# Sample sums by column ranges, conv transposes behind the last product, state transposes ahead of the last products

## The reference

```python
def merge_branches(x, o_cmp, o_sel, o_win, ng, o_fox, ga, gb, p):
    ...
    return x + jnp.einsum('bte,ed->btd', ga * ya + gb * yb, p['w_out'])

def conv_ffn(h, prev_rows, p):
    hn = rms_norm(h, p['norm_ffn_g'])
    u = jnp.einsum('btd,df->btf', hn, p['w_up'])
    g = jnp.einsum('btd,df->btf', hn, p['w_gate'])
    ...
    ue = jnp.concatenate([prev_rows.astype(u.dtype), u], axis=1)
    uc = p['conv_b'] + sum(p['conv_w'][k] * ue[:, k:k + T] for k in range(CONV_W))
    y = jnp.einsum('btf,fd->btd', jax.nn.gelu(uc) * g, p['w_down'])
    return h + y, ue[:, -(CONV_W - 1):]
```

## Time and profile before

| | |
|---|---|
| time, median of 3 runs | 892.27 us (892.04 to 892.54) |
| time of the profiled execution | 892.68 us |
| its span, first to last instruction | 890.8 us |
| mean granted TensorE clock | 0.978 of full |
| TensorE busy | 832.3 us |
| VectorE, ScalarE, GpSimd busy | 513.0, 366.5, 181.6 us |

### The profile page before, as it was taken

How to read it: one execution, slowest core, us unless ns; L and a number is a source line. 1 busy time by engine, 2 the same in 40 slices (tenths; PEclk the granted TensorE clock), 3 DMA queues, 4 the chain that set the end, 5 groups by cost and what they waited for, 6 DMA issues and landing times. The chain is left out here.

```text
span 890.8 us, 18476 instructions
## 1 busy us (share of the span) xinstructions
PE 832.3 (93%) x7479; PEld 682.0 (77%) x7479; DVE 513.0 (58%) x972; ACT 366.5 (41%) x660; POOL 181.6 (20%) x256
## 2 busy tenths in 40 slices
PE   6999887999999999989998788999799999999997
PEld 5999655899889876556554458995598899899885
DVE  6477688434437667635565424647666556656554
ACT  5246655423343244533243404425154344344332
POOL 3000385202210223333343500000011111101010
PEclk9999898999999999999999998999889999999999
DMA  6553495923443599999999988872074455554412
GB/s 204 178 165 120 78 306 206 245 96 104 174 155 139 176 408 356 326 406 390 422 416 395 398 316 229 225 273 94 0 236 143 142 158 194 185 170 141 141 47 64
DMA packets 90644, 192.07 MB, mean 216 GB/s; under 512 B 7467, under 2 KB 68811, under 8 KB 78060
## 3 DMA queue, kind: packets, MB, share of 16 engines
q0 software_dynamic: 15408, 106.04, 30.8%
q1 hardware_dynamic: 74878, 84.05, 30.4%
q10 hardware_dynamic: 288, 0.97, 0.4%
HBM read 187.57 MB, written 7.64 MB: 219 GB/s over the span
## 5 line engine op out<-in xcount | busy, mean ns | idle before, releaser
L1763 PEld LDWEIGHTS banks<-consts_base,stream_rows 128*128 128x128 f32 x672 | 73.2, 141 | 33.9 <-issue 26.9
L2002 ACT ACTIVATE keys_turned<-banks 128x512 f32<-128x512 f32 x94 | 55.1, 597 | 101.0 <-PE banks L1763 100.8
L1763 PE MATMUL banks<-consts_base,stream_rows 128*128 128x128 f32 x672 | 82.7, 276 | 7.4 <-DVE fox_probs_turned L1993 2.6
L261 PE MATMUL banks<-tokens_turned_high,w_gates_high 128*128 128x288 f32 x288 | 86.4, 300 | 2.3 <-PEq L194 2.3
L262 PE MATMUL banks<-tokens_turned_low,w_gates_high 128*128 128x288 f32 x288 | 85.3, 296 | 0.0
L263 PE MATMUL banks<-tokens_turned_high,w_gates_low 128*128 128x288 f32 x272 | 81.6, 300 | 0.0
L1296 PE MATMUL banks<-chunks_turned_high,cmp_w_high 64*128 64x256 f32 (+1 forms) x512 | 76.6, 293 | 3.0 <-ACT cmp_hidden L1390 2.6
L1296 PE MATMUL banks<-chunks_turned_low,cmp_w_high 64*128 64x256 f32 (+1 forms) x512 | 73.5, 280 | 0.0
L1983 DVE COPY keys_turned<-banks 128x512 f32<-128x512 f32 x74 | 50.4, 690 | 33.9 <-PE banks L1763 31.4
L254 DVE TENSOR_TENSOR chunks_turned_low<-banks,chunks_turned_high 128x512 fp32r<-128x512 f32 x64 | 41.0, 684 | 39.5 <-ACT chunks_turned_high L249 39.5
L249 ACT ACTIVATE chunks_turned_high<-banks 128x512 fp32r<-128x512 f32 x64 | 34.8, 596 | 65.1 <-PE banks L1139 63.9
(11 more groups left out here) (460 smaller groups left out, 2109.6 us busy)
## 6 DMA issues: line engine op xcount, KB each, us to landing
w_up_gate<-in_w_up SPq DMA_DIRECT2D x12, 1024.0 KB, 7.4
w_up_gate<-in_w_gate SPq DMA_DIRECT2D x12, 1024.0 KB, 9.8
w_down<-in_w_down SPq DMA_DIRECT2D x12, 1024.0 KB, 5.0
w_in_slot<-in_w_in SPq DMA_DIRECT2D x7, 1424.0 KB, 7.5
w_gates<-in_w_in SPq DMA_DIRECT2D x10, 512.0 KB, 6.7
cmp_w_k<-in_cmp_w_k SPq DMA_DIRECT2D x4, 512.0 KB, 8.7
cmp_w_v<-in_cmp_w_v SPq DMA_DIRECT2D x4, 512.0 KB, 11.0
stream_rows<-in_state_win_k SPq DMA_DIRECT2D x8, 256.0 KB, 9.6
```

The source lines that it names most:

```text
L261: nc.tensor.matmul(out, lh, rh, start=start, stop=False, **kw)
L1763: ins = nc.tensor.transpose(bank(t)[:, q * P:(q + 1) * P], src, ident)
L2002: copy = lambda a, b: nc.scalar.activation(a, b, ACT.Copy)
```

## The change

In the merge the four row groups of bank 4 now hold four column ranges of 256 (`W4`), and each k adds to all four: eight matmuls of 256 columns at each odd k in place of four of 512. Nothing has to be added, so the copy to SBUF and the folds go; ScalarE copies the four groups side by side into `hs`, now 32 x 1024, and VectorE's addition for the sample's rows reads them from SBUF. The conv transposes stand behind the last product, into bank 0, and the two copies of their result behind the norm of tile 1. The up/gate rounding keeps its place and so stands ahead of the sample copies.

In the FFN the same is done to `down_sample`. The kept state gets 32 columns a slice in place of 18 (the rest set to zero by GpSimd), and 24 matmuls by the identity bring it to rows in four row groups of banks 0 and 1, ahead of the last 12 down products instead of behind them; ScalarE makes both copies. `rows_done` counts each column half. ScalarE copies the sample's sums and GpSimd adds them to h. SyncE issues four p_conv stores and then y, the second tile in two halves, and y_sample; ScalarE issues four s_conv stores.

The diff without its unchanged lines, but for a few:

```diff
@@ -2294,7 +2294,8 @@
-        hs = c.wo[:, :, :, :].rearrange("p a j e -> p (a j e)")[:, 0:512]
+        W4 = D // 4
+        hs = wo[1][0:NS, :, :, :].rearrange("p a j e -> p (a j e)")
@@ -2320,7 +2321,7 @@
-        hs_ready, hs_folded = c.sem("h_sample_copied"), c.sem("h_sample_folded")
+        hs_ready = c.sem("h_sample_copied")
@@ -2416,28 +2417,17 @@
                 if k % 2:
-                    for q in range(4):
-                        kk, n = k - 1 + q // 2, q % 2
-                        ins = nc.tensor.matmul(c.ps[4][NS * q:NS * q + NS, :], ms[:, kk, :], wt[kk][:, n * 512:(n + 1) * 512],
-                                               start=(k == 1), stop=(k == KD - 1))
+                    for kk in (k - 1, k):
+                        for q in range(4):
+                            ins = nc.tensor.matmul(c.ps[4][NS * q:NS * q + NS, 0:W4], ms[:, kk, :], wt[kk][:, q * W4:(q + 1) * W4],
+                                                   start=(kk == 0), stop=(kk == KD - 1))
-                    if (n, k) == (0, 5):
-                        pe.wait_ge(conv_in, 48)
-                        nc.tensor.transpose(c.ps[5][:, 0:4 * FT], taps_rows, c.k("ident")[0:4 * FT, 0:4 * FT])
-                        for f in range(FT):
-                            turn = nc.tensor.transpose(c.ps[5][:, 4 * FT + f * 2 * DB:4 * FT + (f + 1) * 2 * DB], st_rows[:, f * P:(f + 1) * P], c.k("ident")[0:2 * DB, 0:2 * DB])
-                        turn.then_inc(conv_turned, 1)
-                    if (n, k) == (0, 3):
-                        pe.wait_ge(hs_ready, 1)
-                        for x in range(2):
-                            fold = nc.tensor.matmul(c.ps[6 + x][0:NS, :], c.k("foldhalf")[:, x * NS:(x + 1) * NS], hs[:, :], start=True, stop=True)
-                        fold.then_inc(hs_folded, 1)
                     if (n, k) == (1, 3):
-                        pe.wait_ge(ffn.taps_ready, 2)
+                        pe.wait_ge(hs_ready, 4)
@@ -2446,6 +2436,11 @@
+            pe.wait_ge(conv_in, 48)
+            nc.tensor.transpose(c.ps[0][:, 0:4 * FT], taps_rows, c.k("ident")[0:4 * FT, 0:4 * FT])
+            for f in range(FT):
+                turn = nc.tensor.transpose(c.ps[0][:, 4 * FT + f * 2 * DB:4 * FT + (f + 1) * 2 * DB], st_rows[:, f * P:(f + 1) * P], c.k("ident")[0:2 * DB, 0:2 * DB])
+            turn.then_inc(conv_turned, 1)
@@ -2497,6 +2492,9 @@
             act.wait_ge(ffn.ug_in[0], 32)
             split_high(nc, ffn.ugh[0][:, :, :, :], ffn.w_ug[0][:, :, :, 0:P]).then_inc(ffn.ug_high, 1)
+            act.wait_ge(wt_done, KD // 2)
+            for q in range(4):
+                nc.scalar.activation(hs[:, q * W4:(q + 1) * W4], c.ps[4][NS * q:NS * q + NS, 0:W4], ACT.Copy).then_inc(hs_ready, 1)
@@ -2559,7 +2557,7 @@
             def add(t, cols, into):
-                sums_h = c.pairs[t if t < 2 else 3][0:r, cols]
+                sums_h = c.pairs[t][:, cols] if t < 2 else hs[:, cols]
@@ -2574,19 +2572,14 @@
-            dve.wait_ge(wt_done, KD // 2)
-            nc.vector.tensor_copy(hs[:, :], c.ps[4][:, :]).then_inc(hs_ready, 1)
-            dve.wait_ge(hs_folded, 1)
+            dve.wait_ge(hs_ready, 4)
-            dve.wait_ge(conv_turned, 1)
-            nc.vector.tensor_copy(ffn.taps[:, :], c.ps[5][:, 0:4 * FT]).then_inc(ffn.taps_ready, 1)
-            nc.vector.tensor_copy(ffn.st[:, :, :], c.ps[5][:, 4 * FT:4 * FT + 2 * DB * FT].rearrange("p (f s) -> p f s", f=FT)).then_inc(ffn.taps_ready, 1)
@@ -2598,6 +2591,9 @@
                 norm(1, half)
+            dve.wait_ge(conv_turned, 1)
+            nc.vector.tensor_copy(ffn.taps[:, :], c.ps[0][:, 0:4 * FT])
+            nc.vector.tensor_copy(ffn.st[:, :, :], c.ps[0][:, 4 * FT:4 * FT + 2 * DB * FT].rearrange("p (f s) -> p f s", f=FT))
             for i, g in enumerate((2, 3)):
@@ -2613,7 +2609,6 @@
-        self.taps_ready = c.sem("conv_taps_ready")
@@ -2651,25 +2646,32 @@
-        ys = c.sb("y_sample_parts", [P, 512], ctx=ctx)
+        ys = c.sb("y_sample", [NS, D], ctx=ctx)
+        W4, FG = D // 4, FT // 4
         taps, st = ffn.taps, ffn.st
-        last = c.sb("conv_new_state", [P, FT, NL], ctx=ctx)
-        last_rows = c.sb("conv_state_and_new_rows", [NL, FF], ctx=ctx)
+        last = c.sb("conv_new_state", [P, FT, NS], ctx=ctx)
+        last_rows = c.sb("conv_state_and_new_rows", [P, FF // 4], ctx=ctx)
-        lcopy_late, rows_done = c.sem("new_state_copied_late"), c.sem("prompt_rows_summed")
+        y_sample_ready = c.sem("y_sample_ready")
+        rows_done, s_stored, p_stored = c.sem("prompt_rows_summed"), c.sem("sample_state_stored"), c.sem("prompt_state_stored")
-        ys_ready, ys_folded, pair_done = c.sem("y_sample_copied"), c.sem("y_sample_folded"), c.sem("sample_products_done")
+        ys_ready, pair_done = c.sem("y_sample_copied"), c.sem("sample_products_done")
         block = ctx.enter_context(nc.Block())
+        def store_state(eng, name, lo, hi, done):
+            eng.wait_ge(lcopy, 2)
+            for k in range(4):
+                eng.dma_start(d[name].rearrange("l b w f -> (l b w) f")[:, k * FF // 4:(k + 1) * FF // 4], last_rows[NS * k + lo:NS * k + hi, :]).then_inc(done, 16)
@@ -2694,16 +2696,18 @@
-            for t in range(QT):
-                sp.wait_ge(y_ready, 2 * t + 2)
-                sp.dma_start(d["y_prompt"].rearrange("b (t p) d -> p (b t) d", p=P)[:, t, :], h[:, t, :]).then_inc(c.stored, 16)
-            sp.wait_ge(y_ready, 6)
+            y_rows = d["y_prompt"].rearrange("b (t p) d -> p (b t) d", p=P)
+            store_state(sp, "p_conv", 0, 2, p_stored)
+            sp.wait_ge(y_ready, 2)
+            sp.dma_start(y_rows[:, 0, :], h[:, 0, :]).then_inc(c.stored, 16)
+            for n in range(2):
+                sp.wait_ge(y_ready, 3 + n)
+                sp.dma_start(y_rows[:, 1, n * 512:(n + 1) * 512], h[:, 1, n * 512:(n + 1) * 512]).then_inc(c.stored, 16)
+            sp.wait_ge(y_sample_ready, 1)
-            sp.wait_ge(lcopy, 4)
-            sp.wait_ge(lcopy_late, 2)
-            sp.dma_start(d["p_conv"].rearrange("l b w f -> (l b w) f"), last_rows[0:2, :]).then_inc(c.stored, 16)
-            sp.dma_start(d["s_conv"].rearrange("l b w f -> (l b w) f"), last_rows[2:NL, :]).then_inc(c.stored, 16)
-            sp.wait_ge(c.stored, 16 * (c.n_stored + 5))
+            sp.wait_ge(c.stored, 16 * (c.n_stored + 4))
+            sp.wait_ge(s_stored, 64)
+            sp.wait_ge(p_stored, 64)
@@ -2714,16 +2718,16 @@
-                    if rows_done:
-                        ins.then_inc(rows_done, 1)
+                        if rows_done:
+                            ins.then_inc(rows_done, 1)
             def down_sample(u, start):
-                for q in range(4):
-                    f, n = q // 2, q % 2
-                    ins = nc.tensor.matmul(c.ps[6][NS * q:NS * q + NS, :], hid[f][:, SEQ:NTOK], w_dn[u][:, f, n * 512:(n + 1) * 512],
-                                           start=start, stop=True, skip_group_check=True)
+                for f in range(2):
+                    for q in range(4):
+                        ins = nc.tensor.matmul(c.ps[6][NS * q:NS * q + NS, 0:W4], hid[f][:, SEQ:NTOK], w_dn[u][:, f, q * W4:(q + 1) * W4],
+                                               start=start and f == 0, stop=True, skip_group_check=True)
@@ -2750,19 +2754,15 @@
+            pe.wait_ge(kept, FT)
+            for g in range(FG):
+                for k in range(4):
+                    ins = nc.tensor.matmul(c.ps[g // 4][NS * k:NS * k + NS, g % 4 * P:(g % 4 + 1) * P], last[:, FG * k + g, :], c.k("ident"),
+                                           start=True, stop=True)
+                if g in (3, FG - 1):
+                    ins.then_inc(lturn, 1)
             pe.wait_ge(hid_low, FT)
             down(1, False, rows_done)
-            pe.wait_ge(ys_ready, 1)
-            for n in range(2):
-                ins = nc.tensor.matmul(c.ps[6 + n][0:NS, :], c.k("foldhalf")[:, n * NS:(n + 1) * NS], ys[:, :], start=True, stop=True)
-            ins.then_inc(ys_folded, 1)
-            pe.wait_ge(kept, FT)
-            for g in range(FT // 4):
-                if g in (2, 4):
-                    pe.wait_ge(y_ready, g)
-                for k in range(4):
-                    ins = nc.tensor.transpose(c.ps[g][0:NL, k * P:(k + 1) * P], last[:, 4 * g + k, :], c.k("ident"))
-                ins.then_inc(lturn, 1)
@@ -2795,15 +2795,21 @@
             loop(act, FT // 4, lambda i: steps(i, split, take))
-            for g in (0, 1, 2, 4):
+            for g in range(2):
-                nc.scalar.activation(last_rows[:, g * 512:(g + 1) * 512], c.ps[g][0:NL, :], ACT.Copy).then_inc(lcopy, 1)
+                cols = slice(512 * g, min(512 * (g + 1), FF // 4))
+                nc.scalar.activation(last_rows[:, cols], c.ps[g][:, 0:cols.stop - cols.start], ACT.Copy).then_inc(lcopy, 1)
+            act.wait_ge(pair_done, FT // 2)
+            for q in range(4):
```

(21 more changed lines are left out.)

## The result

The changed kernel takes 885.32 us (median, 10 runs) against 892.45 us of the kernel before (10 runs, the three shown earlier among them): ratio 0.9929, 95% interval 0.9919 to 0.9938, or 5.5 to 7.2 us less. The forecast was 885.3. The changed kernel again, beside three experiments on the same chip, gave 885.48 and 0.9925 (0.9908 to 0.9943). One execution of a later kernel, the one with another order of the quarters, took 2759.56 us, and the figures given for that kernel are those of its other five.

A forecast was written before the change was run, and what follows sets the result against it. TensorE, busy 93% of the span, was taken as the bound: its work and its waits between stages. 2.04 + 1.87 + 2.9 + 0.3 = 7.1 us less gave a median forecast of 885.3 us, range 883.4 to 888.3.

The forecast's parts named there:

- The folds: Merge, TensorE's product stream: the two folds cost 2.04 us, restart included, and go wholly: -2.04 us.
- The conv transposes: Merge: moved behind the last product they leave the stream, -1.87 us, hidden in TensorE's 3.02 us wait for the norm.
- VectorE in time: Merge: VectorE's chain for tile 0 ends about 627.4, before the turning at about 630.1; slack 2.7 us.
- Column ranges: Merge and FFN sample sums: eight 256-column matmuls cost the same as four of 512: 0, bounds -0.8 to +1.6 us.
- The tail: End of the kernel: the last store is issued earlier, with the same 2.8 us to land: -2.9 us, bounds -1.0 and -3.4.
- The clock: Between merge and FFN: small transposes in the gap affect the granted clock's fall: -0.3 us, bounds -3.0 to +0.9.
- the rule on transposes: Trainium skill: full clock doesn't engage for transposes; by it the gap's transposes keep nothing up, clock term 0, sum 6.8 us.
- the late tail: Rival, kernel end: GpSimd's addition, ScalarE's stores or transfers end last, leaving 1.0 of the 2.9 us: 887.2 us; 15%.
- the dear quarters: Rival, sample groups: each second set of four starts dearly, 0.12 to 0.19 us, 16 times: up to 888.3 us; 9%.
- half a merge: Rival, merge: the sample's path holds VectorE up beyond the 2.7 us slack, 2 us stick out: 887.3 us; 4%.
- the spared clock: Rival, between merge and FFN: the granted clock stays up because the gap is partly filled: 2.2 us less, 883.1 us; 8%.

The follow-up runs named there:

- the second run: The changed kernel itself, unaltered, run again beside three experiments on the same chip: 885.48 us, ratio 0.9925 to the kernel before.
- fillers: The changed kernel with unread matmuls in TensorE's idle times at the merge's end: 883.45 us; with transposes instead of matmuls: 883.93 us.
- the three parts: The kernel before with one part each: conv transposes moved, 889.09 us; merge column ranges without folds, 889.26 us; the FFN's part, 889.25 us.

## Why the prediction was right

The time, 885.3, was met by the measured 885.32; the steps not all alike. That it was met to 0.02 us is luck: the ratio leaves 5.5 to 7.2 us for the gain, and the profiled execution gained 7.7. The two parts of the merge were met by more than luck, each by a kernel of its own; in the tail the number came out near while the reason given with it was not shown, and the clock's 0.3 is not shown at all.

1. The folds: 2.04 forecast, 2.06 alone. Right.
2. The conv transposes: 1.87 forecast, 1.86 alone; 1.36 us of cover left, for 1.2. Right.
3. VectorE in time. Timeline of the changed kernel, VectorE, and ScalarE's table load:

```profile
620.61 1.23 DVE L2561 TENSOR_TENSOR h_rows<-banks,h_rows 128x1024 f32<-128x1024 f32 x1 [3.22 <-PE banks L263]
...
623.16 1.21 DVE L2561 TENSOR_TENSOR h_rows<-w_o,h_rows 32x1024 f32<-32x1024 f32 x1
...
625.74 1.28 DVE L2567 SCALAR_TENSOR_TENSOR h_normed<-h_rows,h_sumsq,ffn_gain 128x1024 f32<-128x1024 f32 x1
...
623.14 1.28 ACT L2501 ACT_TABLE_LOAD   x1
```

The norm ends at 627.0 and the turning starts at 629.85: 2.8 us of slack, for 2.7. The table load ends at 624.42 behind the copies, as forecast, and the root right behind it is done 0.8 us before VectorE wants it. Right.

4. Column ranges: 0 forecast, 0 measured, by L451's rate. The order in the list, which the prediction took from L451 as exactly the new one, isn't what it rests on, as the other order shows.
5. The tail: 2.9 forecast, 2.8 in the first trace, and 2.4 to 3.6 over all kernels that have the change's own tail. The state matmuls took 1.49 for 1.5, GpSimd 2.35 at the upper end of 1.9 to 2.4, ScalarE's issues 0.36 to 0.45 for 0.31, the last issue ended at 879.35 with a landing of 2.7. (The working's own difference, 887.03 less 884.2, is 2.83, which rounds to 2.8 and not to 2.9.) Each row came about as forecast, and yet the explanation beneath was off: I took the last issue and a fixed landing of 2.8 us as what sets the end. SyncE's wait for it was 1.6 to 3.1 us over the kernels with y_sample last, so it isn't fixed, and the end moved by 1.1 us between traces of one and the same tail. That the forecast met the first trace is in part luck. The place of the state matmuls, which the working counts on, gave nothing in the run that undid it together with the order of the stores. One of the signs of being wrong that the prediction names did show: GpSimd's addition ended at 878.93, 0.72 us behind VectorE's last (878.21), over the 0.5 named. It had no price, as the run with the copies first shows.
6. The clock: -0.3 forecast. The first trace has -0.5 in the transposes (1.44 us for 1.97) and -0.2 in the FFN's slow stretch; the second run has 1.97 again and +0.6. Over the six traces of the changed merge without fillers this stretch takes 26.2 to 27.4 us, in the kernel before 26.8, and the transposes 1.97 in four of them. So it is 0 within what runs differ by, inside the bounds of -3.0 and +0.9: the 0.3 is not shown. The slow stretch left behind the FFN's start was 4.1 us in the first trace and 5.9 in the second, where the prediction named anything but 4 to 5 as a sign of being wrong. The granted clock in the first, around its fall and its rise:

```profile
638.00:639.00 1.00, 0.92 (x6) 0.42 (x4) 0.92 (x4) 0.63 (x2) 0.00 (x0) 0.78 0.00 0
...
645.00:646.00 1.00, 1.00 (x8) 1.00 (x8) 0.54 (x1) 0.00 (x0) 0.00 (x0) 0.81 1.09 377
```

The trace had leaned against the rule on transposes, and rightly.

Of the rivals, the late tail, the dear quarters and half a merge are refuted by rows of their own; the spared clock didn't come by itself, but came with fillers and was worth about the 2.2 that it was priced at. The sum of the three parts' medians, 3.4 + 3.3 + 3.3 us, is more than the 7.1 of the whole; the traces, 1.9 + 2.1 + 2.8 to 3.6, add up. The single ratios are too wide to tell these apart.

## What to carry to other kernels

Where one engine never waits, the cost of work placed in its stream is the distance of the starts around it, and removing or moving it pays exactly that, as long as the others' chains have slack: check each of them before the sum. At the end of a kernel take no single trace for the answer: here one and the same tail ended 10.2 to 11.3 us behind the last sample group, about as much as anything tried on it was worth. Storing the largest result in smaller pieces, the first of them earlier, went with the lowest median, but the traces don't show why. And an idle time between stages costs again behind it, through the granted clock; work that can wait, or even fillers, belongs there.

## What the runs showed of the hardware

- Float32 transposes of 128x128 in TensorE's gaps kept the granted clock at 1.00 (2.4 GHz) as well as matmuls did; without fillers it was at 0.50 (1.2 GHz) for 6.8 to 10.2 us around this stage boundary.
- TensorE took the eight sample matmuls of 256 columns as fast where the list has two of one row group behind each other: 1.02 us a group against 1.00.
- GpSimd's addition of 32x1024 took 2.35 to 2.41 us, more than 1.91 for 128x1024 in the earlier trace rows; VectorE took 1.20. Why fewer partitions took longer wasn't tried.
- Most issues of y's stores took 0.33 to 0.46 us, single ones 0.56 to 1.00, also in one of the two traces of the changed kernel (0.91) and not in the other. Why wasn't tried.
- With the same instructions in the tail, the last packets landed up to 1 us later in some traces than in others, and the end of the kernel with them.
